# A 31-tap depthwise convolution on TensorE: 22 diagonal matrices and 9 VectorE taps, or four column tiles of 32 channels fed by a shifted copy

## What is computed

```python
g = glu_a * jax.nn.sigmoid(glu_b)                       # (B, S, 768), columns of hn @ w_in
cb, new_conf = causal_dwconv(st_conf, g, conf_dw)       # y[t, c] = sum_k conf_dw[k, c] * g[t - 30 + k, c]
cb = layernorm(cb + conf_dw_b, conf_ln_g, conf_ln_b)
y_b = jax.nn.silu(cb) @ conf_pw + conf_pw_b
```

## Time and profile before

| | us |
|---|---|
| runs of the kernel: median of 3 (lowest to highest) | 3378.05 (3377.89 to 3422.32) |
| profiled execution, span of the slowest core | 3372.3 |
| spans of the 8 cores in it | 3363.1 to 3372.3 |
| TensorE matmul busy | 3191.6 (95%) |
| VectorE busy | 1719.7 (51%) |
| ScalarE busy | 957.1 (28%) |

### The profile page before, as it was taken

One profiled execution on the slowest core, in us unless ns is written; L12 is line 12 of the kernel. 1 busy time (PEld: TensorE's weight loads), 2 busy tenths in 40 slices (PEclk: granted clock), 3 DMA queues, 4 the chain that ended last, 5 costly groups with the idle time before them and its releaser, 6 DMA issues.

```text
span 3372.3 us, 69283 instructions; the slowest of 8 cores (3363.1 to 3372.3 us)
## 1 busy us (share of the span) xinstructions
PE 3191.6 (95%) x27520; PEld 2702.2 (80%) x27520; DVE 1719.7 (51%) x3111; ACT 957.1 (28%) x1486; POOL 486.4 (14%) x914
## 2 busy tenths in 40 slices
PE   6999999999999999999489999999898999999997
PEld 5888888888888888888377788887677878888786
DVE  5635454525844444544485374465258526456625
ACT  2223232423132322423203142243231324223322
POOL 1111111121011111111001111111110111111110
PEclk9999999999999999999699999999999999999998
DMA  7688989897578899888747889888964688988895
GB/s 145 103 138 143 142 144 155 142 146 113 100 126 144 148 156 145 149 137 140 195 85 112 139 145 152 137 147 170 174 111 80 112 149 141 146 135 151 148 170 116
DMA packets 149437, 466.35 MB, mean 138 GB/s; under 512 B 21760, under 2 KB 26624, under 8 KB 148096
## 3 DMA queue, kind: packets, MB, share of 16 engines
q0 software_dynamic: 133856, 425.83, 77.7%
q1 hardware_dynamic: 15264, 36.10, 3.3%
HBM read 869.70 MB, written 17.94 MB: 263 GB/s over the span
## 4 chain that ended last, share of the span: by engine, by line
PE 90%; DMA 4%; DVE 3%; issue 1%; ACT 1%; SPq 0%; DVEq 0%; POOL 0%; ACTq 0%; POOLq 0%
PE ps L121 90%; DVE U L121 2%; DMA wb<-w_down 2%; DMA h<-xT 1%; DVE xn L121 1%; DMA wb<-w_out 1%; DMA wb<-w_in 0%; DMA wb<-w_up 0%; ACT U L121 0%; DVE cat L121 0%; ACT rstd L121 0%; ACT cat L121 0%; SPq L121 0%; DVE h L121 0%; DVEq L117 0%
## 5 line engine op out<-in xcount | busy, mean ns | idle before, releaser
L121 PE MATMUL ps<-xn,wb 128*128 128x264 bf16 (+1 forms) x17664 | 2053.3, 279 | 34.2 <-DVE xn L121 29.0
L121 PEld LDWEIGHTS ps<-xn,wb 128*128 128x128 bf16 x17664 | 1733.5, 98 | 336.3 <-issue 40.2
L121 DVE SCALAR_TENSOR_TENSOR U<-U,cstt 128x528 f32<-128x528 f32 x944 | 724.9, 768 | 520.7 <-ACT U L121 459.0
L121 PE MATMUL ps<-U,wb 128*128 128x264 bf16 (+1 forms) x5920 | 688.2, 279 | 27.4 <-DMA wb<-w_down 26.7
L121 PEld LDWEIGHTS ps<-U,wb 128*128 128x128 bf16 x5920 | 581.6, 98 | 131.5 <-issue 30.0
L121 ACT ACTIVATE U<-ps 128x528 f32<-128x528 f32 (+1 forms) x420 | 259.5, 618 | 1359.7 <-PE ps L121 904.9
L121 DVE TENSOR_TENSOR h<-ps,h 128x528 f32<-128x528 f32 (+1 forms) x320 | 228.3, 715 | 667.2 <-PE ps L121 667.2
L121 POOL DMA_DIRECT2D wb<-w_up x352 | 187.0, 531 | 1068.2 <-PE ps L121 1022.4
L121 ACT ACTIVATE U<-ps,cstt 128x528 f32<-128x528 f32 (+2 forms) x364 | 250.8, 689 | 106.3 <-DVE U L121 106.3
L121 PE MATMUL ps<-cat,wb 128*128 128x264 bf16 (+1 forms) x2048 | 234.6, 277 | 6.9 <-ACT cat L121 4.7
L121 ACT ACTIVATE U<-U 128x544 f32<-128x544 f32 (+5 forms) x276 | 197.7, 718 | 144.8 <-DVE U L121 144.3
(11 more groups left out here) (53 smaller groups left out, 893.2 us busy)
## 6 DMA issues: line engine op xcount, KB each, us to landing
wb<-w_up POOLq DMA_DIRECT2D x352, 512.0 KB, 6.7
wb<-w_down POOLq DMA_DIRECT2D x256, 352.0 KB, 5.8
wb<-w_in POOLq DMA_DIRECT2D x136, 512.0 KB, 5.7
wb<-w_out POOLq DMA_DIRECT2D x64, 512.0 KB, 9.4
wb<-ple_gate POOLq DMA_DIRECT2D x64, 512.0 KB, 6.0
h<-xT SPq DMA_DIRECT2D x8, 1056.0 KB, 13.8
wb<-conf_pw POOLq DMA_DIRECT2D x24, 192.0 KB, 3.6
yT<-xn SPq DMA_DIRECT2D x2, 2112.0 KB, 8.1
```

The source lines that it names most:

```text
L121: ins = getattr(e, name)(*a, **kw)
```

## The change

The convolution of a group is written with t = 4r + s: output = sum over r (8) and s (4) of w[30 - 4r - s] times g shifted by 4r + s. For each of the four blocks cg of 32 channels, a tile rep holds on its 128 partitions four copies of the 32 rows, copy s shifted by s columns. One matmul with 128 rows and 32 columns of weights (four stacked 32 x 32 diagonals, d4) then does four taps of 32 channels; four such matmuls, for cg = 0 to 3, write the four blocks of 32 partitions of one PSUM bank. A convolution has 8 x 2 x 4 = 64 matmuls in place of 44, and VectorE has no taps.

rep is written by 16 DMAs per group from Gb, issued by SyncE one after another (dmas records a list of them with one wait ahead of the first and one common token). rep and d4 each have two buffers. The eviction with the bias goes to ScalarE. conf_dgen writes 32 x 32 = 1024 elements per group and stands ahead of conf_pair(j). D is gone, tmpc shares memory with U_a[1], the constants grow from 1296 to 1572 columns.

```diff
+    def dmas(self, eng, fns, sem, reads=(), writes=()):
+        waits = self._waits(eng, self._deps(reads, writes, ()))
+        for fn in fns:
+            self.cnt[sem] = self.cnt.get(sem, 0) + 16
+            self.q[eng].append((_record(fn), waits, (sem, 16)))
+            waits = []
...
+        rep_t = sb("rep", [128, 2, 4, 30 + WMAX], BF16)
+        d4_t = sb("d4", [128, 2, 8, 4, 32], BF16)
...
+            for i in range(2):
+                S.op("dve", (lambda e, i=i: e.memset(rep_t[:, i, :, :].rearrange("p a b -> p (a b)"), 0.0)), writes=[repB[i]])
...
                     def conf_dgen(j):
-                        wo = COFF["cdw"] + (l * 6 + j) * 31
-                        wbc = cst_t[:, wo + NDT:wo + 31].unsqueeze(2).broadcast_to([128, 31 - NDT, 128])
-                        idb = ident_v.unsqueeze(1).broadcast_to([128, 31 - NDT, 128])
-                        S.op("dve", (lambda e: e.tensor_tensor(out=D_a[:, NDT:31, :], in0=idb, in1=wbc, op=ALU.mult)), reads=[B["cst"]], writes=[DB])
+                        i2 = j % 2
+                        o4 = COFF["cd4"] + (l * 6 + j) * 32
+                        wbc = cst_t[:, o4:o4 + 32].unsqueeze(2).broadcast_to([128, 32, 32])
+                        idb = id4_v.unsqueeze(1).broadcast_to([128, 32, 32])
+                        S.op("dve", (lambda e: e.tensor_tensor(out=d4_t[:, i2, :, :, :].rearrange("p r c m -> p (r c) m"), in0=idb, in1=wbc, op=ALU.mult)),
+                             reads=[B["cst"]], writes=[D4B[i2]])
+
+                    def conf_rep(j):
+                        i2 = j % 2
+                        Gb = Gb_a[i2]
+                        fns = []
+                        for s_ in range(4):
+                            n_ = 30 + (W if s_ == 0 else WP - s_)
+                            for cg in range(4):
+                                fns.append(lambda e, s_=s_, cg=cg, n_=n_: e.dma_start(
+                                    out=rep_t[32 * s_:32 * s_ + 32, i2, cg, s_:s_ + n_], in_=Gb[32 * cg:32 * cg + 32, 0:n_]))
+                        S.dmas("sp", fns, f"s_rep{i2}", reads=[GbB[i2]], writes=[repB[i2]])
 
                     def conf_conv(j):
...
-                        S.op("dve", (lambda e: e.tensor_scalar(out=CB_a[:, j, 0:WP], in0=G[:, 0:WP], scalar1=cst_t[:, wo:wo + 1], scalar2=None, op0=ALU.mult)),
-                             reads=[GB[i2], B["cst"]], writes=[CBBj[j]])
-                        for k in range(1, NDT):
-                            S.op("dve", (lambda e, k=k: e.scalar_tensor_tensor(out=CB_a[:, j, 0:WP], in0=G[:, k:k + WP], scalar=cst_t[:, wo + k:wo + k + 1],
-                                                                                in1=CB_a[:, j, 0:WP], op0=ALU.mult, op1=ALU.add)),
-                                 reads=[GB[i2], B["cst"]], writes=[CBBj[j]])
...
                         def fn(e):
-                            order = [30] + list(range(NDT, 30))
-                            for n_, k in enumerate(order):
+                            for r in range(8):
                                 for t in range(2):
                                     lo = t * Wh
-                                    hi = (t + 1) * Wh if k == 30 else min((t + 1) * Wh, WP)
-                                    e.matmul(ps_t[:, 2 * slot + t, 0:hi - lo], lhsT=D_a[:, k, :], rhs=Gb[:, k + lo:k + hi],
-                                             start=(n_ == 0), stop=(n_ == len(order) - 1))
-                        S.op("pe", fn, reads=[DB, GbB[i2]], writes=[psb[slot]])
+                                    hi = (t + 1) * Wh if r == 0 else min((t + 1) * Wh, WP)
+                                    for cg in range(4):
+                                        e.matmul(ps_t[32 * cg:32 * cg + 32, 2 * slot + t, 0:hi - lo], lhsT=d4_t[:, i2, r, cg, :],
+                                                 rhs=rep_t[:, i2, cg, 30 + lo - 4 * r:30 + hi - 4 * r], start=(r == 0), stop=(r == 7))
+                        S.op("pe", fn, reads=[D4B[i2], repB[i2]], writes=[psb[slot]])
                         bias_ = cs("cdb", l * 6 + j)
...
+                        S.op("act", (lambda e: e.activation(out=v2(CB_a[:, j, 0:W]), in_=psv(slot), func=AF.Identity, bias=bias_)),
+                             reads=[psb[slot], B["cst"]], writes=[CBBj[j]])
...
                     conf_dgen(0)
                     conf_pair(0)
+                    conf_rep(0)
                     for j in range(1, 6):
+                        conf_dgen(j)
                         conf_pair(j)
                         conf_conv(j - 1)
-                        conf_dgen(j)
+                        conf_rep(j)
                     sc_triple(0)
                     conf_conv(5)
```

More of the change, by code:

```diff
@@ L102, in dma @@
         return tok
+    def dmas(self, eng, fns, sem, reads=(), writes=()):
[4 more added lines that the diff above has]
+            waits = []
+        tok = (sem, self.cnt[sem])
+        self._mark(tok, reads, writes)
+        return tok
     def wait(self, eng, deps):
@@ L126, in _pack_consts @@
     segs = [("nmix", L * 16), ("nffn", L * 16), ("nple", L * 16), ("nfin", 16), ("pscale", L * 4),
-            ("cdw", L * 6 * 31), ("cdb", L * 6), ("lng", L * 6), ("lnb", L * 6), ("pwb", L * 6),
-            ("scw", L * 6 * 3), ("ffw", L * FC * 2 * 3), ("invc", 64), ("ident", 128)]
+            ("cdw", L * 6 * 30), ("cd4", L * 6 * 32), ("id4", 32), ("cdb", L * 6), ("lng", L * 6), ("lnb", L * 6), ("pwb", L * 6),
+            ("scw", L * 6 * 3), ("ffw", L * FC * 2 * 3), ("invc", 64)]
     off, o = {}, 0
@@ L183, in build_nc @@
         rstd_t = sb("rstd", [128, WMAX])
-        NU = 14848 + 1024 + 224 + 448
+        NU = 14096
+        rep_t = sb("rep", [128, 2, 4, 30 + WMAX], BF16)
+        d4_t = sb("d4", [128, 2, 8, 4, 32], BF16)
         U_t = sb("U", [128, NU])
         ps_t = es.enter_context(nc.psum_tensor("ps", [128, 8, 512], F32))
-        dma_sems = ["s_y0", "s_y1", "s_hx0", "s_hx1", "s_hx2", "s_hx3", "s_h", "s_ptb", "s_wpl", "s_cst", "s_ptw", "s_ost0", "s_ost1", "s_stp", "s_stc", "s_sts", "s_stf"] + [f"s_w{i}" for i in range(NWB)]
+        dma_sems = ["s_y0", "s_y1", "s_hx0", "s_hx1", "s_hx2", "s_hx3", "s_h", "s_ptb", "s_wpl", "s_cst", "s_ptw", "s_ost0", "s_ost1", "s_stp", "s_stc", "s_sts", "s_stf", "s_rep0", "s_rep1"] + [f"s_w{i}" for i in range(NWB)]
         sems = {n: es.enter_context(nc.semaphore(n)) for n in list(ENGS) + dma_sems}
@@ L263, in program @@
             S.op("dve", lambda e: e.memset(ones_f[:], 1.0), writes=[B["onesf"]])
+            repB = [Buf("rep0"), Buf("rep1")]
+            D4B = [Buf("d40"), Buf("d41")]
+            for i in range(2):
+                S.op("dve", (lambda e, i=i: e.memset(rep_t[:, i, :, :].rearrange("p a b -> p (a b)"), 0.0)), writes=[repB[i]])
             for pi in range(2):
@@ L324, in sq_region @@
                         return xn_t, (lambda k: [xnB[k // 2]])
-                    if region == "top":
-                        return sqtop_v, (lambda k: [B["sqtop"]])
                     return cat_t, (lambda k: [catB[k // 2]])
@@ L427, in program @@
                     U_a = [ar.f32(15 + WMAX) for _ in range(2)]
+                    tmpc_a = U_a[1][:, 0:16 * 29].rearrange("p (b s) -> p b s", b=16)
                     S_a = [ar.f32(15 + WMAX) for _ in range(2)]
@@ L443, in program @@
                     dB = [Buf("d0"), Buf("d1")]
-                    ident_v = cs("ident", 0, 128)
+                    id4_v = cs("id4", 0, 32)
                     prez = dict(zip((4, 10, 5), linear_multi([(w_in, l * 34 + 4), (w_in, l * 34 + 10), (w_in, l * 34 + 5)])))
@@ L496, in conf_conv @@
-                        S.op("pe", fn, reads=[DB, GbB[i2]], writes=[psb[slot]])
-                        bias_ = cs("cdb", l * 6 + j)
[L498 to L502, removed]
-                            S.op("act", (lambda e: e.activation(out=CB_a[:, j, WP:W], in_=ps_t[:, 2 * slot + 1, WP - Wh:Wh], func=AF.Identity, bias=bias_)),
-                                 reads=[psb[slot], B["cst"]], writes=[CBBj[j]])
-                        else:
-                            S.op("dve", (lambda e: e.scalar_tensor_tensor(out=v2(CB_a[:, j, 0:W]), in0=psv(slot), scalar=bias_, in1=v2(CB_a[:, j, 0:W]),
-                                                                          op0=ALU.add, op1=ALU.add)), reads=[psb[slot], B["cst"]], writes=[CBBj[j]])
@@ L510, in conf_conv @@
                             S.op("dve", (lambda e: e.tensor_tensor(out=tmpc_a, in0=stc_t[:, j, 0:29, :].rearrange("p s b -> p b s"), in1=wb2, op=ALU.mult)),
-                                 reads=[B["stc"], B["cst"]], writes=[tmpB])
-                            S.op("dve", (lambda e: e.tensor_reduce(out=r1_a, in_=tmpc_a, axis=AX.X, op=ALU.add)), reads=[tmpB], writes=[tmpB])
+                                 reads=[B["stc"], B["cst"]], writes=[UB[1]])
+                            S.op("dve", (lambda e: e.tensor_reduce(out=r1_a, in_=tmpc_a, axis=AX.X, op=ALU.add)), reads=[UB[1]], writes=[tmpB])
```

(11 more changed lines are left out.)

10 lines of the change are left out of this document (1 added, 9 removed).

## The result

The changed kernel is slower: 1.0132 times the kernel before, interval 1.0078 to 1.0185. On the 3378 us of the kernel before that is some 3423 us. That is less than the 2% at which the prediction calls a change, but clear of the scatter. Forecast were 3370 us and no change. The runs of the changed kernel took 3419.6 to 3442.2 us; the eight spans of the profiled one are 3394.1 to 3433.5 us, where they were 3363.1 to 3372.3 us. In some executions cores of one die run at a lower clock and take longer, which leaves out one run of 3562.1 us and is why cores 2 and 3 here are 15 to 22 us longer outside the stages of the convolution too. The other six lie at 3394.1 to 3412.7 us.

A forecast was written before the change was run, and what follows sets the result against it. TensorE, 95% busy, was taken as the bound. Terms -151.5 (work, waits, slow clock gone) + 62.4 (new matmuls) + 59 (copy waits) + 22 (clock) gave -8 us: 3370 us, no change; range 3315 to 3485 us.

The forecast's parts named there:

- What goes, 151.5 us: TensorE, four convolution stages: old convolutions 120.2 us, waits for VectorE 23.5 and slow clock 7.8 would go.
- TensorE's new work, c = 2.6 us: TensorE's 64 column-tile matmuls per convolution, tiles side by side: 2.6 us each, 62.4 us for 24 convolutions.
- low end of 2.05: Lowest time taken for a convolution's 64 load and matmul pairs on TensorE: 2.05 us, 49 us in all.
- both rivals on serial tiles: TensorE's column tiles run one after another: 3450 us, chance 0.12; weight loads don't hide either: 3497 us, chance 0.10.
- The copy's length L = 12.45 us: From a pair's last matmul to its copy in rep: 2.35 to Gb, 6.6 of issues, 3.5 of landing; 59 us of waits.
- the clock, 5.6 us per stage: TensorE's slow clock behind waits for the copy: 5.5 us per stage, 22 us over four stages.
- the prediction's own sign of being wrong: Wrong if convolution 0 doesn't wait for its copy, waits over 13 us, or 64 matmuls take over 4 us.
- The late copy: Rival: copy DMAs share engines with weights, issues 0.70 us apart, landing 8.0 us; 161 us of waits, 3485 us, chance 0.13.

The follow-up runs named there:

- copy_twice_only: Changed kernel with the copies into rep made only for groups 0 and 1 of the first stage, later convolutions rereading them: ratio 0.9731 to the kernel before.
- four_wide: Changed kernel with each group's copy made by 4 DMAs of 128 partitions in place of 16 of 32, same bytes: ratio 0.9876 to the kernel before.

## Why the prediction was wrong, step by step

- *What goes, 151.5 us.* Right as far as the runs can tell: with the copy's cost nearly out (copy_twice_only) the stages fall from 388 to 300 us, 88 us, with one awaited copy of 16.6 us and the clock behind it still in. The sum of terms for that kernel is -151.5 + 47 + 17 + about 2 = -86.
- *TensorE's new work, c = 2.6 us.* It is 1.94 us, below the low end of 2.05. The tiles run side by side, so both rivals on serial tiles fall. The rule on weight loads from the packing section of "TensorE: Matmul & The Clock Gate" in the Trainium skill doesn't hold here: six loads and four matmuls on the same 128 rows begin within 0.03 us (the window 79.83:79.86). The switching off of the fast weight load under column tiling, which the Trainium skill has among the restrictions of "TensorEngine Tiling (Array Packing)" and not in its performance section, cost nothing that the trace shows.
- *The copy's length L = 12.45 us: the step that failed, a term that was mis-sized.* The mechanism was the right one: which convolutions wait (0, 2 and 4, with 1, 3 and 5 free) came out as worked through, and so did the clock, 5.6 us per stage where 5.5 was taken. The time between issues was taken as 0.44 us and is 0.67, so 15 of them take 10 us for 6.6. The landing was taken as 3.5 us; for the copies that are waited for it is 3.7 to 6.5 us on core 3, 4.7 in the mean, and 2.4 to 6.5 on all cores. L is 2.35 + 10 + 4.7 = 17 us.
- *What follows from it.* A wait at convolutions 2 and 4 is L - 7.4 - c: 17 - 7.4 - 1.94 = 7.7 us, measured 8.2 and 8.1 in the mean, forecast 2.45. An error of 4.6 us in L and 0.7 in c made it more than three times as long. Convolution 0 waits 12.0 to 16.5 us for 9.85, and with that the prediction's own sign of being wrong, a wait over 13 us, is there. In sum the waits are 119 us for 59, 60 more, and TensorE's new work is 47 us for 62, 15 less: +37 us where -8 was forecast. That the error in c made up for a quarter of the error in L was luck.
- *The late copy*, the rival on the other side, named this mechanism and priced it at 161 us of waits, with the spacing of 0.70 us that the earlier trace rows also has and a landing of 8.0 us. The measured case lies between it and the forecast. I set the spacing near the two short values, taken from issues whose length varied from 0.34 to 0.71 us, with the reason that the new DMAs are narrower; four_wide shows that the number of rows has no part in it. And the earlier trace rows shows only part of its two bursts. The trace of the kernel before also has in them

```profile
2335.56 0.34 SPq L121 DMA_DIRECT2D pst<-ost  x1
...
2337.18 0.77 SPq L121 DMA_DIRECT2D oss<-sts  x1
2338.04 0.70 SPq L121 DMA_DIRECT2D ofs<-stf  x1
...
3189.48 1.54 SPq L121 DMA_DIRECT2D oss<-sts  x1
3191.12 0.58 SPq L121 DMA_DIRECT2D ofs<-stf  x1
```

so that the steps are 0.39, 0.47, 0.76 and 0.86 us in the first burst and 0.39, 0.70, 0.57 and 1.64 in the second. All eight steps have a mean of 0.72 us, near the 0.67 that was measured, where 0.44 was taken from the lower end. The point from which the change loses, L of 13 us, was only half a microsecond above what I took.

## What to carry to other kernels

A chain of many small DMAs costs per issue, here 0.6 to 0.7 us each on SyncE from 35 to 139 KB. Count them, multiply by the mean spacing of whole bursts in the trace and not by the shortest, add the landing beside the traffic of that stretch, and compare the sum with the work of the other engines ahead of the consumer. What exceeds it is a wait, and the lower clock behind the waits comes on top (here 119 and 22 us). Cover put ahead of a DMA is worth less if it brings transfers of its own: here 11 us of it took 3.5 us off the wait at convolution 0. If a change frees an engine near by, ask first whether that engine can do the copy: here VectorE alone or VectorE and ScalarE, 16 copies of 32 partitions in 4.7 to 6.3 us, turned a loss of 1.3% into a gain of up to 3%.

## What was not expected of the hardware

- Four column tiles of 32 at 264 columns: 64 matmuls with 64 weight loads in 1.94 us, 3.8 times the rate of full matmuls (0.114 us each); 16 passes at 0.114 us would be 1.8 us.
- VectorE and ScalarE write a block of 32 partitions from another block: 0.40 us on VectorE and 0.73 us on ScalarE for some 558 bf16 columns, from start to start. The four of VectorE's 16 copies that stay in their own block take as long as the twelve that don't (0.30 us each without the gap to the next).
- SyncE's issue of a DMA between two tiles takes 0.6 us, for 35 KB as for 139 KB. One of 35 KB lands in 1.9 us with little beside it and in 10.6 us (the median) among seven weight loads.
